# Gate table stored by sets of 64 tokens, with a new order of the scan's gates, of the step from up to down products, and of the end

## The reference, cut to what matters

```
z = h @ w_in ; za = shift(za)
wl = w0 + tanh(lw) @ w2 ; decay = exp(-exp(-softplus(-wl) - 0.5)) ; a = sigmoid(a0 + la @ a2)
y_fwd, s_f = rwkv7_scan(r, w, k, v, kk, a, s0_f, False) ; the same backward
# peer(h): 8 heads, 16 of 16384 experts each
gates = softmax(top_s)
act = gelu(einsum('nd,nhkd->nhk', x, expert_u[idx]))
out = einsum('nhk,nhkd->nd', act * gates, expert_v[idx])
x = x + gt2 * rmsnorm(out, g_post2)
```

## Time and profile before

| what | us |
|---|---|
| median of 3 runs | 3051.0 |
| the profiled execution's own time | 3054.4 |
| its span | 3052.6 |
| PE busy | 2863.6 (94%) |
| DVE busy | 2139.9 (70%) |
| ACT busy | 1192.5 (39%) |
| GpSimd busy | 845.9 (28%) |
| DMA | 815.71 MB, mean 267 GB/s |

### The profile page before, as it was taken

One profiled execution on the slowest core, in us unless ns is written; L12 is line 12 of the kernel. 1 busy time (PEld: TensorE's weight loads), 2 busy tenths in 40 slices (PEclk: granted clock), 3 DMA queues, 4 the chain that ended last, 5 costly groups with the idle time before them and its releaser, 6 DMA issues.

```text
span 3052.6 us, 62528 instructions
## 1 busy us (share of the span) xinstructions
PE 2863.6 (94%) x25834; PEld 2591.6 (85%) x25834; DVE 2139.9 (70%) x3021; ACT 1192.5 (39%) x1749; POOL 845.9 (28%) x552
## 2 busy tenths in 40 slices
PE   7899999899999899889999999999998999999997
PEld 5799998577777769789989999999996878777786
DVE  2455522666565553559977888887777989999897
ACT  3333333333333333343335555553333334433343
POOL 0000000122222220047774444441122442443331
PEclk9999999799999989999999999999998999999998
DMA  9533333233334323245568999999999999999995
GB/s 406 230 124 124 125 134 115 85 131 116 117 137 154 141 100 112 81 170 211 207 222 331 363 398 394 388 404 404 409 393 394 418 418 418 418 418 418 416 418 230
DMA packets 207696, 815.71 MB, mean 267 GB/s; under 512 B 81520, under 2 KB 101104, under 8 KB 118416
## 3 DMA queue, kind: packets, MB, share of 16 engines
q1 hardware_dynamic: 105040, 527.71, 45.2%
q0 software_dynamic: 36864, 268.45, 21.2%
q10 hardware_dynamic: 65600, 16.78, 2.4%
HBM read 772.50 MB, written 40.37 MB: 266 GB/s over the span
## 4 chain that ended last, share of the span: by engine, by line
PE 27%; DMA 14%; DVE 9%; issue 4%; POOL 3%; ACT 1%; SPq 1%; DVEq 0%; ACTq 0%; POOLq 0%
DMA work<-act_table 12%; PE ps L1850 6%; PE ps L1852 6%; PE ps L1851 6%; POOL wlo L1840 3%; DVE x L2346 2%; DVE work L2441 2%; DMA x<-u_rows,idx 2%; PE ps L2203 1%; PE ps L2107 1%; DVE wlo L1840 1%; PE ps L2204 1%; PE ps L2205 1%; PE ps L2109 1%; PE ps L2108 1%
## 5 line engine op out<-in xcount | busy, mean ns | idle before, releaser
L1850 PE MATMUL ps<-hhi,whi 128*128 128x256 f32 x2048 | 588.8, 287 | 24.1 <-POOL wlo L1840 16.2
L1851 PE MATMUL ps<-hlo,whi 128*128 128x256 f32 x2048 | 581.3, 284 | 0.0
L1852 PE MATMUL ps<-hhi,wlo 128*128 128x256 f32 x2048 | 581.2, 284 | 0.0
L2203 PE MATMUL ps<-whi,hhi 128*128 128x512 f32 x1024 | 402.7, 393 | 32.2 <-DVE hlo L2424 18.0
L1850 PEld LDWEIGHTS ps<-hhi,whi 128*128 128x128 f32 x2048 | 394.7, 193 | 29.3 <-POOL wlo L1840 19.0
L2204 PE MATMUL ps<-wlo,hhi 128*128 128x512 f32 x1024 | 400.5, 391 | 0.0
L2205 PE MATMUL ps<-whi,hlo 128*128 128x512 f32 x1024 | 400.2, 391 | 0.0
L2236 POOL DMA_INDIRECT work<-expert_v,idx x128 | 271.1, 2118 | 461.2 <-DVE work L2441 439.3
L1851 PEld LDWEIGHTS ps<-hlo,whi 128*128 128x128 f32 x2048 | 395.0, 193 | 0.0
L1852 PEld LDWEIGHTS ps<-hhi,wlo 128*128 128x128 f32 x2048 | 394.6, 193 | 0.0
L2236 POOL DMA_INDIRECT x<-u_rows,idx x128 | 236.3, 1846 | 443.8 <-DVE x L2346 248.3
(11 more groups left out here) (357 smaller groups left out, 5444.2 us busy)
## 6 DMA issues: line engine op xcount, KB each, us to landing
raw<-expert_u SPq DMA_DIRECT2D x94, 1024.0 KB
x<-w_ada SPq DMA_DIRECT2D x64, 1024.0 KB, 6.3
work<-expert_v SPq DMA_DIRECT2D x64, 1024.0 KB
raw<-expert_v SPq DMA_DIRECT2D x64, 1024.0 KB
raw<-w_in SPq DMA_DIRECT2D x50, 1024.0 KB, 4.8
raw_more<-expert_u SPq DMA_DIRECT2D x34, 1024.0 KB
z<-w_ada SPq DMA_DIRECT2D x32, 1024.0 KB, 13.7
raw<-w_out SPq DMA_DIRECT2D x16, 1024.0 KB, 4.8
```

The source lines that it names most:

```text
L1850: pe.matmul(bank, whi[:, r, k, :], moving_hi, start=(k == 0), stop=False)
L1851: pe.matmul(bank, whi[:, r, k, :], moving_lo, start=False, stop=False)
L1852: last = pe.matmul(bank, wlo[:, r, k, :], moving_hi, start=False, stop=(k == KD - 1))
L2203: pe.matmul(bank, ah, vh[:, part], start=first, stop=False)
```

## The change

Three parts are reordered, and the table's form in DRAM changes.

*Scan*: `front_sums` and `front_gates` go by kind, not by direction: first the two `sg`, then the two `aa`. The `sg` sigmoids stand between ACT's second and third copy of turned factors. The fifth w_ada block moves into level 4.

```
                 gates.wait(pe, it, n - 1)
-            r = slice(64 * (n // 2), 64 * (n // 2) + 64)
-            gates_in.inc(pe.matmul(ps[:, banks[n % 2], 0:T], lora[r, n % 2, :], z[r, (Z_LW, Z_LA)[n % 2], :], start=True, stop=True))
-
-        def front_gates(act, it, d, banks=(6, 7)):
-            gates_in.wait(act, it, 2 * d + 1)
-            gates.inc(nc.scalar.activation(sg[d][:, :], ps[:, banks[0], 0:T], ACT.Sigmoid, bias=colr("w0", it, PAIRS * d)))
-            gates_in.wait(act, it, 2 * d + 2)
-            gates.inc(nc.scalar.activation(aa[d][:, :], ps[:, banks[1], 0:T], ACT.Sigmoid, bias=colr("a0", it, PAIRS * d)))
+            r = slice(64 * (n % 2), 64 * (n % 2) + 64)
+            gates_in.inc(pe.matmul(ps[:, banks[n % 2], 0:T], lora[r, n // 2, :], z[r, (Z_LW, Z_LA)[n // 2], :], start=True, stop=True))
+
+        def front_gates(act, it, half, banks=(6, 7)):
+            for d in range(2):
+                gates_in.wait(act, it, 2 * half + d + 1)
+                gates.inc(nc.scalar.activation((sg, aa)[half][d][:, :], ps[:, banks[d], 0:T], ACT.Sigmoid,
+                                               bias=colr(("w0", "a0")[half], it, PAIRS * d)))
 
         def front_factors(act, it, d):
...
-            ADA_EARLY, ADA_LEVELS = 5, (1, 2, 3)
+            ADA_EARLY, ADA_LEVELS = 4, (1, 2, 3, 4)
             ADA_LATE = len(ADA_LEVELS)
...
                         if g == 2:
                             ada_sums(it, 0)
                         tn_ready.inc(nc.scalar.activation(tn[:, g], tiled(ps[:, INIT_BANK[g], 0:T]), ACT.Copy))
-                    if more:
-                        operands.wait(act, it, 2)
-                        halves.wait(act, it, 2)
-                        front_gates(act, it + 1, 0)
+                        if more and g == 1:
+                            operands.wait(act, it, 2)
+                            halves.wait(act, it, 2)
+                            front_gates(act, it + 1, 0)
...
                         turned.inc(last)
 
                     toks_ready.wait(pe, it, 3)
-                    ada(it, 4)
                     turn_first(0)
```

```
-        gate_table = nc.dram_tensor("gate_table", [P, NK + PAD, LAT], F32, kind="Internal").ap()
+        gate_table = nc.dram_tensor("gate_table", [P, SETS, NK + PAD, GT], F32, kind="Internal").ap()
...
-        gate_in = carve(fb_, 2, 2, LAT)
+        gate_in = carve(fb_, 2, SETS, 2, GT)
...
 
+                def groups(r, at):
+                    sp.dma_start(gate_in[:, r], gate_table[:, :, bass.ds(at, 2), :]).then_inc(gate_landed[r].sem, 16)
+                    sp.dma_start(act_in[:, r].rearrange("p e t -> p (e t)"),
+                                 act_table[:, bass.ds(at, 2), :].rearrange("p e t -> p (e t)")).then_inc(gate_landed[r].sem, 16)
...
+                    sp.wait_ge(spilled[r].sem, 16 * 2)
+                groups(0, 0)
                 load_v(expert_v[0], 0)
                 load_v(expert_v[1], 1)
                 spill(NK - 4)
+                groups(1, 2)
...
-                    act.dma_start(gate_table[:, 0:NK, s * GT:(s + 1) * GT], stage[:, s % 2]).then_inc(stage_out[s % 2].sem, 16)
+                    act.dma_start(gate_table[:, s, 0:NK, :], stage[:, s % 2]).then_inc(stage_out[s % 2].sem, 16)
...
+                def gate(it, j):
+
+                    r = j % 2
+                    dve.wait_ge(gate_landed[r].sem, it * 32 + 32 * (j // 2) + 32)
+                    by_set = act_in[:, r].rearrange("p e (s t) -> p s e t", s=SETS)
+                    nc.vector.tensor_tensor(by_set, by_set, gate_in[:, r], ALU.mult).then_inc(gated_.sem, 1)
+
+                def lower(it, j):
+                    dve.wait_ge(act_high.sem, it * 2 + (j + 1))
+                    nc.vector.tensor_tensor(act_lo[:, j % 2], by_tile(act_in[:, j % 2]), act_hi[:, j % 2].bitcast(F32), ALU.subtract
+                                            ).then_inc(act_split.sem, 1)
+
...
```

```
-
-                act.wait_ge(gated_.sem, 1)
-                act.wait_ge(prod.sem, M_DOWN)
-                nc.scalar.activation(act_hi[:, 0], act_in[:, 0], ACT.Copy).then_inc(act_high.sem, 1)
+                    if n == 2:
+                        act.wait_ge(gated_.sem, 1)
+                        nc.scalar.activation(act_hi[:, 0], by_tile(act_in[:, 0]), ACT.Copy).then_inc(act_high.sem, 1)
                 act.wait_ge(ug_used.sem, SLOTS)
                 nc.scalar.activation(dots[:, :], dots[:, :], ACT.Gelu_apprx_tanh).then_inc(weights_in.sem, 1)
...
+                    if n == 1:
+                        gate(0, 0)
+                    if n == 2:
+                        lower(0, 0)
                 gate(0, 1)
-                lower(0, 0)
```

```
+                sum_squares(0)
+                root(1, 1)
+                evict(0, 2)
+                root(0, 3)
+                sum_squares(1)
+                root(2, 5)
+                evict(1, 6)
...
+                pe.wait_ge(ctx_scaled.sem, ctx_scaled.v + 1)
+                for g in range(4):
+                    pe.wait_ge(evicted.sem, g + 1)
+                    for i in range(4):
+                        k = 4 * g + i
+                        last = pe.transpose(ps[:, g, i * P:(i + 1) * P], accs[:, k * P:(k + 1) * P], table("ident"))
+                    last.then_inc(turned_back.sem, 1)
+                pe.wait_ge(evicted.sem, 8)
+                for j in range(KD // 2):
+                    if j >= 4:
+                        pe.wait_ge(added_back.sem, j - 3)
+                    for i in range(2):
+                        k = 2 * j + i
+                        for tile in range(2):
+                            last = pe.transpose(ps[:, (4 + j) % 8, (2 * i + tile) * P:(2 * i + tile + 1) * P],
+                                                done_tok[:, tile, k * P:(k + 1) * P], table("ident"))
+                    last.then_inc(turned_back.sem, 1)
+                reduced(0, 1)
+                inverted(1, 2)
+                dve.wait_ge(vg_used.sem, SLOTS)
+                nc.vector.scalar_tensor_tensor(out=vg[0], in0=accs[:, :], scalar=1.0, in1=accs[:, :], op0=ALU.mult, op1=ALU.mult,
+                                               accum_out=tok_sum[:, 0:1]).then_inc(scale_ready.sem, 1)
+                inverted(0, 3)
+                dve.wait_ge(scale_ready.sem, 4)
+                nc.vector.tensor_scalar(accs[:, :], accs[:, :], tok_sum[:, 0:1], None, ALU.mult).then_inc(ctx_scaled.sem, 1)
+                reduced(1, 4)
+                inverted(2, 5)
...
```

More of the change, by code:

```diff
@@ L714, in front_step @@
                 if k == 0:
-                    gates.wait(dve, it, 2 * d + 1)
+                    gates.wait(dve, it, d + 1)
                     if d:
@@ L735, in front_step @@
                 if k == 0:
-                    gates.wait(dve, it, 2 * d + 2)
+                    gates.wait(dve, it, d + 3)
                     fc.done(nc.vector.tensor_scalar(kd[d][:, :], aa[d][:, :], colr("k_a", it), ka1[:, bass.ds(it, 1)], ALU.mult, ALU.add))
@@ L1827, in build_program @@
         stores_y = sem("stores_y")
+        ctx_scaled = Tally(vn_turned.sem, HB)
         def raw_at(m):
@@ L2219, in _ @@
                 down(NK // 4 - 1, 3, last=True)
-                srcs = [lambda k: accs[:, k * P:(k + 1) * P], lambda k: done_tok[:, 0, k * P:(k + 1) * P],
-                        lambda k: done_tok[:, 1, k * P:(k + 1) * P]]
-                pe.wait_ge(evicted.sem, 9)
[L2224 to L2228, removed]
-                        for i in range(4):
-                            last = pe.transpose(ps[:, n % 8, i * P:(i + 1) * P], srcs[tile](k + i), table("ident"))
-                        last.then_inc(turned_back.sem, 1)
+                pe.wait_ge(ctx_scaled.sem, ctx_scaled.v + 1)
[15 more added lines that the diff above has]
+                    last.then_inc(turned_back.sem, 1)
             @block.gpsimd
@@ L2412, in _ @@
                         rest(it, n)
-                for n in range(REST - TURNS * TURN_OF):
-                    rest(TURNS, n)
                 def gate(it, j):
@@ L2480, in _, with reduced @@
-                dve.wait_ge(x_back.sem, 16)
-                for k in range(0, KD, 4):
-                    for tile in range(TILES):
-                        n = (k // 4) * TILES + tile
-                        dve.wait_ge(turned_back.sem, n + 1)
-                        for i in range(4):
-                            part = x[:, k + i, tile * P:(tile + 1) * P]
-                            last = nc.vector.scalar_tensor_tensor(
-                                out=part, in0=ps[:, n % 8, i * P:(i + 1) * P],
-                                scalar=mod[:, 80 + k + i, (1 if tile else 0):(2 if tile else 1)], in1=part,
-                                op0=ALU.mult, op1=ALU.add)
-                        last.then_inc(added_back.sem, 1)
+                def reduced(tile, done):
+                    dve.wait_ge(squares_done.sem, done)
```

(25 more changed lines are left out.)

66 lines of the change are left out of this document (24 added, 42 removed).

## The result

The changed kernel takes 3065.2 us (median of 22 runs, 3059.4 to 3071.6), the kernel before 3055.3 us beside it (22 runs, 3042.5 to 3071.9): ratio 1.0028, 95% interval 1.0016 to 1.0040, so it is slower by 0.3%. I had forecast 3031 us, faster, with a range that ended at 3054. The profiled execution took 3070.1 us with a span of 3068.3.

| us | before | after | difference | forecast |
|---|---|---|---|---|
| first up product starts | 1325.8 | 1301.1 | -24.7 | -24 |
| first to last up product | 959.0 | 993.4 | +34.4 | +2 |
| last up to first down product | 18.5 | 6.1 | -12.4 | -16 |
| first to last down product | 720.1 | 747.3 | +27.2 | +26 |
| last down product to the end of the span | 29.2 | 20.4 | -8.8 | -8 |

What follows compares the result with a forecast made beforehand. Limits taken: PE's order and short waits in the scan, PE and DMA in scatter, DMA in down, a chain of small steps last. Terms -24 + 2 - 2 + 12 - 8 = -20 gave 3034.4 profiled, 3031 us median; range 3012 to 3054.

Steps and rivals of the forecast that it cites:

- Scan, -24: Scan: shorter waits for w_ada and sigmoids and fewer clock dips save 24 us, bounds -10 and -31.
- the clock's six dips: Scan: clock halves behind waits in six of eight pairs, 9.8 us in all; most should go, counted as 4.
- Stores, +2 (-7 to +18): Gate table stores in the scatter stage: 32 KB rows for 256 B ones cost 2 us net, bounds -7 and +18.
- the slack is about 9 us in the scatter stage: Scatter stage: block needed 15 us after its load is issued, takes some 6 us, so slack is about 9 us.
- the lump: Gate table store: may come as one lump of 10.1 us in which u blocks and gathers stand.
- a turn of up to 64 descriptors: DMA queues: skill's rule that engines alternate queues by packets up to 64 descriptors; the new store would be one turn.
- Rival 3: Gate table stores: each stops PE for 5 us, +18 in place of +2, 3047 us; chance 0.08.
- Rival 4: Gate table reads: 512 B reads keep the light price of 46.7 ns, +49 for +12, 3068 us; chance 0.07.
- Up to down, -2: Up to down products: PE gains 16 us in the gap, but DMA limits what lasts to -2, bounds -20 and 0.
- Reads, +12: Gate table reads, mostly in the full stage: 512 B runs at 27.6 ns each cost 12 us, bounds 0 and +49.
- The rule that 512 B is line rate: Gate table reads: skill gives 512 B as least transfer at line rate; by that the reads' term is 0.
- End, -8: End of kernel: reordered closing steps let the last store land near 3044.3, saving 8 us, bounds -5 and -10.

Runs made afterwards that it cites:

- e9: Changed kernel with the gate table laid out by pairs of rows: stores in 512 B runs, whole, reads in 2 KB runs; 3016.2 us.
- e1: Changed kernel with the gate table of before: stores in 256 B runs, whole, reads in 2 KB runs; 3025.3 us.
- e12: e9 with the way from up to down products as before, groups read only after the last spill has landed; 3016.9 us.
- e8: e4 with each spill of activations issued ahead of the expert_v row and group reads in front of it, from up to down; 3034.5 us.
- e4: Changed kernel with each 4 MB store cut into eight 512 KB pieces of 4 KB runs, issued over several steps; 3032.7 us.
- e6: Changed kernel with store runs of 8 KB in place of 32 KB, issued at the same moment; 3054.8 us.
- e3: Changed kernel with store runs of 2 KB in place of 32 KB, issued at the same moment; 3037.6 us.
- e13: Changed kernel, first three stores cut into eight pieces of 16 neighbouring partitions with 32 KB packets, last store as in e4; 3068.5 us.
- e15: e13 with each piece taking every eighth partition in place of 16 neighbours; 3041.0 us.
- e5: Changed kernel with the gate table of before, each store of 256 B runs cut into eight pieces; 3045.7 us.

## Why the prediction was wrong, step by step

- **Scan, -24.** Right: -24.7, and both waits that were to go are gone. DVE's mask is late next as said (0.57 us for 0.6), level products start 7.1 us after the scores for 7.5; the wait for the last two copies is 1.15 us where I had 0.3, and four of the clock's six dips went. With none left, in e9 and e1, the scan gave 28.6 and 29.1 us.
- **Stores, +2 (-7 to +18).** Wrong: +34.4, and +32.0 with the table alone. This is the step that failed: "the slack is about 9 us in the scatter stage". It was worked out for the blocks of expert_u, and no engine waited for one. The tightest is another transfer on the same queue: a spill goes out behind a block, in rows of 1 KB, and its buffer is wanted again two products (13.6 us) later; it took 21 us. The gathered rows took 18 to 21 us for some 10. Second, I gave the lump 10.1 us in which others stand; it lasts 14 us and more, since the others keep their turns, each a packet. And each stop takes clock with it: the granted clock is 0.50 (1.2 GHz) in the 4 us or so behind each, where a product starts every 0.21 us for 0.12. PE's waits for low parts grew by 25.7 us (6.9 to 32.6), and what is left of the 34.4, 8.7, goes with that clock.
- The rule I quoted of the Trainium skill ("DMA: Bandwidth & Descriptors", section "Queues, rings and completion order"), a turn of up to 64 descriptors, made me expect one turn. The trace does not agree: 133, 121 and 148 packets of three queues in the same 14 us, and nearly equal counts in parts of 4 us, are turns of about one row. That the rule gave 99 us for the old store's 98.4 was an agreement of the totals and no test of the turns. Rival 3 had the right mechanism; its 5 us a stop are 5.6 to 9.1 us of waiting and 34.4 / 4 = 8.6 with all. Rival 4's 3068 is close to the 3065.2 measured by luck: it had the reads at 46.7 ns a row, and they cost 31.
- **Up to down, -2.** Right in the sum (gap and down: e12 against e9, +0.7 us) and off in a step: PE's gap is 6.1 us, not 2, and a spill behind two blocks of expert_v and the reads of the first two pairs of groups landed after 20.7 us, which left a hole in the transfers (0.51 of the DMA at 2310). e8 shows that the hole cost nothing: the bytes bound the stage anyway.
- **Reads, +12.** Right: +12.0 with the table alone; in company e4 against e9 says 16.2 in the down stage. By the queues a row of 512 B costs (0.589 x 8000 - 11,167 x 0.3162 - 5,583 x 0.0874) / 22,334 = 31 ns, for my 27.6. The rule that 512 B is line rate (Trainium skill, same page, "Specifications") doesn't hold here: 417 GB/s over 2400 to 2900 us became 410.
- **End, -8.** Right: -8.8.

With +34.4 for +2 the sum is +12.4; measured on the spans it is +15.7, and the rest is the gap and the down stage, +14.8 together for a forecast of +10.

## What to carry to other kernels

Before a transfer is made faster by longer packets, ask what stands on the other queues, and take the slack of the tightest small transfer, not of the big ones. A background store wants to be slow: packets of 2 KB or less here, or pieces spread over time, and all of it landed before its buffer is wanted. Packets as long as its neighbours' 8 KB rows still cost 24 us of up stage when they came at once. Where bytes bound the next stage, closing a gap of TensorE ahead of it gave nothing (e8, e12).

## What the runs showed of the hardware

- While several queues had work, the share of the store's queue fell with the size of its packets down to 2 KB and hardly below: 69.7% of the engines at 32 KB (the changed kernel), 39.6% at 8 KB (e6), 30.7% at 2 KB (e3), 31.7% at 512 B (e9), 28.8% at 256 B (e1), each over 14 us that begin some 3 us behind the issue of the first store.
- A row of 32 KB took 3.0 us of an engine when a transfer took 16 neighbouring partitions (e13) and 1.26 us when it took every eighth (e15). All transfers together moved 365, 345 and 345 GB/s in the three 100 us from 1700 us with the first, 387, 389 and 366 with the second.
- Issuing a second transfer of 2,048 packets of 256 B right behind the first took 14.4 to 17.2 us in each of three sets, and ScalarE stood for up to 15.7 us (e5).
- In the full down stage rows of 512 B took 31 ns of an engine each, and all transfers fell from 417 to 410 GB/s.
